# A decoder layer on one core: the evacuation order of its last head round, and the attention output staged through two buffers instead of eight

## The reference

```
xn = rms_norm(x); proj = xn @ w_in                # q,k,v | mlstm q,k,v,i,f,o | two gates
oa = rms_norm(diff_attention(qa, ka, va))         # 8 heads, causal, 128 wide
ob = sigmoid(ml_o) * rms_norm(mlstm_chunkwise(...))
merged = g[0] * (oa @ w_proj_a) + g[1] * (ob @ w_proj_b)
h = x + merged @ w_out
h = h + (relu(rms_norm(h) @ w_ff1) ** 2) @ w_ff2
return rms_norm(h)
```

## Time and profile before

| what | value |
|---|---|
| device time, median of three | 1974.37 us |
| profiled execution: time, span | 1974.37 us, 1972.6 us |
| TensorE busy | 1910.6 us, 97% |
| VectorE, ScalarE, GpSimd busy | 60%, 49%, 19% |
| mean granted TensorE clock | 0.997 |
| last head round and tail (about) | 851 to 1067 us |

### The profile page before, as it was taken

The page is one execution under the profiler, slowest core; times in us unless marked ns, Lnnn a source line. Parts: engine busy times, 40 slices in busy tenths (PEclk is TensorE's granted clock), DMA queues, the critical chain, the costliest instruction groups (busy, mean ns, idle before and its releaser), DMA issues. The chain is left out here.

```text
span 1972.6 us, 26074 instructions
## 1 busy us (share of the span) xinstructions
PE 1910.6 (97%) x9378; PEld 1598.0 (81%) x9378; DVE 1190.3 (60%) x1538; ACT 965.5 (49%) x1634; POOL 383.9 (19%) x211
## 2 busy tenths in 40 slices
PE   5999999999999999989999999999999999999998
PEld 4788888788888787878888888888888888888886
DVE  6755666566575757553412112278777677789874
ACT  4355565556465556544434322226666765533341
POOL 4221212112121121211213444440000000021002
PEclk9999999999999999999999999999999999999999
DMA  5562747554444546274446453655686686563422
GB/s 152 87 179 57 162 68 152 78 131 107 119 108 115 117 68 166 57 160 99 65 97 213 134 154 92 222 187 211 208 297 225 223 298 211 209 231 132 159 82 86
DMA packets 207826, 291.79 MB, mean 148 GB/s; under 512 B 36841, under 2 KB 127593, under 8 KB 200833
## 3 DMA queue, kind: packets, MB, share of 16 engines
q1 hardware_dynamic: 195856, 282.21, 51.6%
q10 hardware_dynamic: 11888, 8.49, 1.3%
HBM read 203.56 MB, written 87.10 MB: 147 GB/s over the span
## 5 line engine op out<-in xcount | busy, mean ns | idle before, releaser
L730 PE MATMUL gp<-r1h,w_hi 128*128 128x512 f32 x1152 | 454.6, 395 | 6.0 <-ACT ev L1076 3.7
L732 PE MATMUL gp<-r1h,w_lo 128*128 128x512 f32 x1152 | 450.0, 391 | 0.0
L731 PE MATMUL gp<-r1l,w_hi 128*128 128x512 f32 x1152 | 449.4, 390 | 0.0
L1973 POOL TENSOR_TENSOR w_lo<-w_raw,w_hi 128x1024 fp32r<-128x1024 f32 x87 | 218.3, 2510 | 852.2 <-ACT w_hi L1071 852.2
L730 PEld LDWEIGHTS gp<-r1h,w_hi 128*128 128x128 f32 x1152 | 216.8, 188 | 49.7 <-issue 4.1
L732 PEld LDWEIGHTS gp<-r1h,w_lo 128*128 128x128 f32 x1152 | 216.5, 188 | 46.2
L731 PEld LDWEIGHTS gp<-r1l,w_hi 128*128 128x128 f32 x1152 | 216.9, 188 | 41.8
L991 PE MATMUL scores<-xh,qh 128*128 128x512 f32 x512 | 200.1, 391 | 0.6 <-ACT res L1372 0.6
L995 PE MATMUL scores<-xh,ql 128*128 128x512 f32 x512 | 199.2, 389 | 0.0
L993 PE MATMUL scores<-xl,qh 128*128 128x512 f32 x512 | 199.2, 389 | 0.0
L1214 ACT ACTIVATE pr<-scores,nb 128x256 f32<-128x256 f32 (+7 forms) x128 | 93.8, 738 | 118.3 <-DVE nb L1607 116.7
(11 more groups left out here) (342 smaller groups left out, 3745.5 us busy)
## 6 DMA issues: line engine op xcount, KB each, us to landing
xraw<-xo_d SPq DMA_DIRECT2D x54, 1024.0 KB, 5.2
proj_d<-ev SPq DMA_DIRECT2D x128, 256.0 KB, 4.3
rq<-in_w_ff SPq DMA_DIRECT2D x32, 1024.0 KB, 7.8
w_raw<-in_w_in SPq DMA_DIRECT2D x56, 512.0 KB, 9.0
xo_d<-res SPq DMA_DIRECT2D x78, 256.0 KB, 3.3
xo_d<-ring SPq DMA_DIRECT2D x60, 256.0 KB, 2.9
pr<-proj_d SPq DMA_DIRECT2D x16, 512.0 KB, 5.4
gt<-proj_d SPq DMA_DIRECT2D x32, 256.0 KB, 2.8
```

The costliest lines, as they stand in the source:

```text
L730: pe.matmul(gp[half][:], wh[slot][:, k, :], mh[:, k, t], start=(k == 0), stop=False)
L731: pe.matmul(gp[half][:], wh[slot][:, k, :], ml[:, k, t], start=False, stop=False)
L732: mm = pe.matmul(gp[half][:], wl[slot][:, k, :], mh[:, k, t], start=False, stop=(k == KT - 1))
L1973: pool.tensor_tensor(wl[slot][:], raw[slot][:], wh[slot][:].bitcast(F32), ALU.subtract).then_inc(w_split, 1)
```

## The change

Three edits.

1. **Last round, ScalarE:** of the units of a slot only all but the last are copied out ahead of `attend`; the last is copied behind it (in slot 0 inside it, between the splits of k and q). In an odd slot, which has one unit, this moves its only `evac`.
2. **SP in the last round:** `row_loads` of head 7 (two loads of 512 KB) are issued at j = 2 instead of j = 3, that is ahead of the two stores of block N_GATE+1.
3. **Tail:** `oa_d` is read through `stg[0]` and `stg[1]`, the load of tile k waiting until VectorE has done the lo part of tile k-2. The loads stand one step later in SP's list, pairs at j = 13, 14, 15 and, for tiles 6 and 7, behind the loop and ahead of the stores of block N_GATE+14. ScalarE takes hi k right behind `evac` of unit 24+k, one earlier than before. The first two loads of `ob_d` now wait on `stg_lo` as well.

```diff
+STAGE_AT = {12: (0, 1), 13: (2, 3), 14: (4, 5), 15: (6, 7)}
...
             def stage_in(k, src):
                 if k >= KT + 2:
                     sp.wait_ge(stgb_lo, k - KT - 1)
+                else:
+                    wait(sp, stg_lo, k - 1)
                 sp.dma_start(stg[k % 2][:], src).then_inc(stg_in[k % 2], 16)
...
-            def oa_load(k):
-                sp.dma_start(res[:, k, :], oa_d[k]).then_inc(x_in[k], 16)
...
             for j in range(16):
-                store(N_GATE + j - 2, oa_loads if j == 14 else None)
+                store(N_GATE + j - 2)
                 gate_load(j + 2)
-                if j == 15:
-                    oa_load(6)
-                    oa_load(7)
                 if j == 13:
                     sp.wait_ge(oa_st, 16 * NH)
                     sp.wait_ge(ob_st, 16 * NH)
-                    oa_load(0)
-                    oa_load(1)
+                for k in STAGE_AT.get(j - 1, ()):
+                    stage_in(k, oa_d[k])
...
-                if j == 3:
+                if j == 2:
                     row_loads(NH - 1)
+            for i in STAGE_AT[15]:
+                stage_in(i, oa_d[i])
...
-                for k in GATE_UNITS_AT[s]:
+                for k in GATE_UNITS_AT[s][:-1]:
                     evac(N_GATE + k // 2, k % 2)
-                attend(NH - 1, s, lambda: None)
+                def evac_units():
+                    for k in GATE_UNITS_AT[s][-1:]:
+                        evac(N_GATE + k // 2, k % 2)
+                attend(NH - 1, s, evac_units)
+                if s:
+                    evac_units()
...
                 for i in range(2):
                     evac(n, i)
-                    if 2 * (j - 12) + i:
-                        stage_hi(2 * (j - 12) + i - 1)
-            stage_hi(KT - 1)
+                    for k in STAGE_AT.get(j, ())[i:i + 1]:
+                        stage_hi(k, r2h)
```

More of the change, by code:

```diff
@@ L391, in wload_head, with store @@
                     wload(n, b % 2, col_block(w_in2, h * P + off))
-            def store(n, behind=None):
+            def store(n):
                 for i in range(2):
@@ L398, in store @@
                                  ev[i][:]).then_inc(st[i], 16)
-                    if behind:
-                        behind(i)
             def head_src(h, b):
@@ L955, in wo_step @@
                     pe.wait_ge(x_out, 2 * TT + (2 * (i - 1) + half + 1 if i else 0))
-                    pe.wait_ge(x_in[i], 48)
+                    pe.wait_ge(x_in[i], 32)
                     for j in range(4):
@@ L1279, in _, with stage_hi @@
                         split_hi(n + 1, (n + 1) // 2, (n + 1) % 2)
-                for k in GATE_UNITS_AT[s]:
+                for k in GATE_UNITS_AT[s][:-1]:
                     evac(N_GATE + k // 2, k % 2)
-                attend(NH - 1, s, lambda: None)
[L1284 to L1288, removed]
+                def evac_units():
[4 more added lines that the diff above has]
+                    evac_units()
+            def stage_hi(k, to):
                 act.wait_ge(stg_in[k % 2], 16 * (k // 2 + 1))
-                act.activation(r1h[:, k, :], stg[k % 2][:], ACT.Copy).then_inc(stg_hi, 1)
+                act.activation(to[:, k % KT, :], stg[k % 2][:], ACT.Copy).then_inc(stg_hi, 1)
             for j in range(12, 16):
@@ L1306, in _ @@
                 if j < KT:
-                    stageb_hi(j)
+                    stage_hi(KT + j, r1h)
                 else:
@@ L1707, in _ @@
                 dve.wait_ge(stg_hi, k + 1)
-                dve.tensor_tensor(r2l[:, k, :], res[:, k, :], r2h[:, k, :].bitcast(F32), ALU.subtract).then_inc(stg_lo, 1)
+                dve.tensor_tensor(r2l[:, k, :], stg[k % 2][:], r2h[:, k, :].bitcast(F32), ALU.subtract).then_inc(stg_lo, 1)
             for j in range(2 * KT):
```

## The result

The changed kernel takes 1992.68 us (median of 11 executions) against 1977.36 us for the kernel before (11 executions): ratio 1.0079, 95% interval 1.0066 to 1.0091, that is 15.6 us slower (13.1 to 18.0).

The account below looks back on a forecast made before the run. TensorE, busy 97% of the span, was taken to bound the kernel. Copies behind attend 5.7 us plus tail 6.4 us made 12.1 us on 1974.37 us, forecasting 1986.5 us, range 1978 to 1996.

Parts of the forecast that it names:

- The copy behind attend, 5.7 us: Last round: odd slots' copies end too late in slots 7, 9, 13, by 1.9, 2.2 and 1.6 us; sum 5.7 us.
- No slow clock behind a wait of 2 us: Last round: the only clock drop followed 3.7 us of idle, so none was taken for waits of 2 us.
- Row loads, 0: Last round, SP: row loads one step earlier put 1 MB ahead of two stores; taken as 0, up to 4 us.
- Tail, unit 27: 4.1 us and 1.5 of slow clock: Tail: hi 0 waits for tile 0 ahead of unit 25's copy; unit 27 4.1 us late, 5.6 with slow clock.
- The ring, 12.2 us a turn: Tail: two-buffer cycle of tile loads, hi copies and weight splits takes 12.2 us against TensorE's 10.9; unit 31 5.8 us late.
- The last store: 3 us to land, unit 32 at 7.1 us late: Tail end: a store behind tiles 6 and 7 lands in 3 us, holding unit 30's copy; unit 32 starts 7.1 us late.
- 6.4 us taken instead of the 7.1 worked out: Tail total: 6.4 us taken, staying low because the next stage's stg loads land in 5.4 us (median).
- the lower bound: Tail: first landing 1.7 us earlier, fewer loads crowding the weight load, gives a tail cost of 5.4 us.
- Short landings: Rival: tail loads land sooner, tail costs 0, 1979.4 us, chance 0.12; with the first stall gone 1974.2 us, 0.05.
- ScalarE did not run ahead: Rival: ScalarE finishes 2 us sooner in slots 7, 9, 13, so only the tail costs; 1980.8 us, chance 0.10.
- The ring did not drag: Rival: landings of 9.3 us in both tail turns, or row loads stretching the first stall; 1995.4 us, chance 0.18.
- All that the stretch could give back: 5.9 us: Stretch, 851 to 1067 us: unit 4's stall worth 5.2 us plus 0.7 weight split wait; no gain counted.

Follow-up runs that it names:

- e5: Changed kernel with only the odd slots' copies put back ahead of attend; even slots keep their last copy behind it: ratio 1.0046 to the kernel before.
- e2: Kernel before plus edit 1 alone (last copy of each slot behind attend, in slot 0 inside it): ratio 1.0057 to the kernel before.
- e12: Second measurement of the kernel before plus edit 1 alone (last copy of each slot moved behind attend, in slot 0 inside): ratio 1.0039.
- e4: Changed kernel with the store of unit 28 issued ahead of tile 6 and that of unit 29 ahead of tile 7: ratio 1.0062 to the kernel before.
- e6: Changed kernel with the loads of tiles 0 to 5 ahead of their step's weight load instead of behind it: ratio 1.0026 to the kernel before.
- e7: Changed kernel with stores of units 28 and 29 ahead of tiles 6 and 7 respectively, and hi k one copy later: ratio 1.0040 to the kernel before.
- e11: Kernel before with only the copy of slot 9 moved behind attend: ratio 1.0021 to the kernel before.
- e3: Kernel before plus edit 2 alone, head 7's two row loads one step earlier: ratio 1.0007 to the kernel before.
- e1: Changed kernel with edit 1 undone, all copies of a slot ahead of attend again: ratio 1.0058 to the kernel before.
- e9: Kernel before with unit 1's copy inside slot 0's attend, head 7's mLSTM loads one step later, tiles 0 and 1 ahead of block 15's weight load: 0.9961, 1971.01 us.
- e10: Changed kernel, two buffers kept: copies ahead of attend except slot 0, row loads back at j = 3, mLSTM loads later, tiles ahead of weight loads: ratio 0.9964.
- e8: Kernel before with head 7's two mLSTM input loads one step later, behind the stores of gate units 0 and 1: ratio 1.0000.

## Why the prediction was right, and where a term was off

Slower was forecast, and slower it is: 1986.5 us forecast, 1992.68 measured, inside the range of 1978 to 1996. Of the 6.2 us between the two, some 3 are the base: the sum starts from 1974.37 us, the median of three executions, and the kernel before measured 1977.36 over eleven. The rest is the change itself, 12.1 us forecast and 15.6 measured. In the profiles it is 16.6, or 4.5 above the sum: 0.2 in the round, 0.7 of a tail chosen too low, 1.1 for a later unit 32 and 2.5 for the slow clock behind it.

- *The copy behind attend, 5.7 us.* Right in place and size: 1.64, 2.07 and 1.76 us ahead of units 13, 16 and 22 against 1.9, 2.2 and 1.6; 5.9 us for the round with some tenths of slower matmuls; no cost in slot 5 and in even slots (e5). Not foreseen: 0.8 us more ahead of unit 28 when the tail is as before (e2, e12).
- *No slow clock behind a wait of 2 us.* Held in the changed kernel's profile and in those of e2, e4 and e12, not in those of e6, e7 and e11, which lose 1.7 us behind unit 16. The bound "plus a slow clock" belonged into the sum with some weight.
- *Row loads, 0.* Held (e3), up to a wait of 0.4 us that shows when nothing else is late.
- *Tail, unit 27: 4.1 us and 1.5 of slow clock.* 3.74 and about 1.7. Tile 0 landed in 11.9 us, taken as 12.2.
- *The ring, 12.2 us a turn.* 11.7 and 11.9. It did not make units 29 and 31 wait in the changed kernel, where the slow unit 27 had given it time, but does where that unit is quick (e1, e5); unit 31 is 4.5 us late within the tail, 5.8 were forecast.
- *The last store: 3 us to land, unit 32 at 7.1 us late.* This is the term that was mis-sized. The store stands behind the tiles 6 and 7 and took 5.7 us. So the wait ahead of unit 32 is 3.8 us where 1.3 were forecast (7.1 less 5.8), and unit 32 came 8.2 us late within the tail. And behind that wait the clock fell, as it does behind the one at unit 4, for another 2.5 us. I had applied that only at unit 27. The tail costs 10.8 us.
- *6.4 us taken instead of the 7.1 worked out.* Neither reason held. The 5.4 us of the later `stg` loads is no less than the 5.2 us that the ring was already given, so it speaks for no lower figure; and the weight load, which the lower bound took to be quicker with fewer tiles behind it, took 11.1 us as before. That choice moved the number the wrong way.
- *Rivals.* Short landings: the mechanism exists, but for the tiles that matter only when the order in the queue is changed (e6: tile 0 landed in 3.3 us). In the changed kernel itself tile 6, issued when all before it had landed, took 3.2 us, but no unit waits for it. I had worked out 3.2 us from the Trainium skill (DMA: Bandwidth & Descriptors, Anatomy of one DMA), which fits GpSimd's path; these two loads on SP's queue agree with that estimate. ScalarE did not run ahead. The ring did not drag beyond its stated turn.
- *All that the stretch could give back: 5.9 us.* e9 and e10 are 5.9 us shorter. But the cause given for unit 4's wait was half of it: with the two mLSTM loads out of the store's way (e8), the split of block 2 holds the unit.

The view of tiles 6 and 7 in the changed kernel, 1073.5 to 1076.5 us:

```profile
DMA to landing us min/median/max: 3.2/4.3/5.4
```

That each of these waits stems from its stated cause is shown by the runs that take it away: e1 and e5 for units 13 to 22, e4 for unit 32, e6 and e7 for unit 27. For unit 4 it takes three: with the split early and the store late (the changed kernel) and with the store sooner and the split late (e8) a wait stays, with both moved (e9) it is gone. Left open is why the granted clock falls behind some waits and not behind others at the very same place.

## What to carry to other kernels

When an engine that works through a fixed list copies results out for TensorE, look up for each copy when its bank is wanted next, and what stands ahead of it in the list: a copy may stand behind work only if that work ends in time, and never behind a wait for a load with a finished unit behind it. In SP's list the order of issue was also the order of landing, in this stretch of every profile here: put a small urgent load or store ahead of a slow strided one, and two buffers do what eight did. When a wait disappears on removing its cause and the time stays, read the new wait in the same place, since the second cause may be close behind the first (0.2 us in e8).

## What the hardware showed that I had not expected

- A 512 KB load (128 rows of 4 KB) with nothing in the queue ahead of it landed in 3.2 us (tile 6 in the changed kernel), and with only a store about to land in 3.3 (e6); the same load behind one weight load of the same size took 11.9 to 12.2 us, because that weight load itself (128 columns out of a wide matrix) took 11.1 us. It took as long with two tiles behind it as with six, and still 10.5 us with the two tiles ahead of it, landed 3.2 us after its issue (e10, first view). Yet the weight load one block before, of the same shape, took 5.7 us in the changed kernel (second view). Why one is twice as slow as the other is open.

```profile
DMA to landing us min/median/max: 10.5/10.5/10.5
```
```profile
DMA to landing us min/median/max: 5.7/5.7/5.7
```

- The granted clock fell to 0.50 to 0.73 over 5 us behind waits of 3.6 us in most profiles, though not in e4 at unit 4. Behind waits of 1.9 us at one and the same place (unit 16) it fell in three profiles (e6, e7, e11) and stayed at 1.00 in four (the changed kernel, e2, e4, e12). The length of the wait alone does not decide: it stayed at 1.00 behind 2.7 us ahead of unit 27 (e1, e5) and fell to 0.66 behind 2.2 us ahead of unit 4 (e8). A fall cost 1.5 to 3.0 us beside the wait.
- Identical code ahead of the stretch took between 0.5 and 4.3 us more than in the first profile, so a difference of 5 us between two profiled spans says nothing. The same stretch between two matmuls repeats to a few tenths where the clock does the same in both (e2 and e12: 6.7 and 6.9 us), and is off by the cost of a fall where it does not.
